# Decoder block on one core: S5's angle fractions of blocks 1 to 7 on GpSimd, another order of sums in bc's first half, and a begin with the first weight unit in halves

## The chip, the core and the metric

The kernel runs on one core of a Trainium2 chip. The metric is the device time of one execution in microseconds (us). TensorE (PE in the rows, PEld its weight loads), VectorE (DVE), ScalarE (ACT) and GpSimd (POOL) each work through a queue of their own in order and wait for one another on semaphores. SyncE (SP) issues most of the DMAs.

## The reference

A decoder block on 256 tokens of 2048 channels. The change touches the first RMSNorm with the product behind it, and the S5 mixer:

```python
hn = rmsnorm(h, norm_mix_w)
z, xbc, dt_raw, u, g_a, g_b = split(hn @ w_in)
...
def s5_mixer(u, lam_re, lam_im, log_dt, b_re, b_im, c_re, c_im, d_skip, w_glu):
    lam_bar = exp(lam * dt)                      # 64 groups x 64 states
    bu = einsum("gpc,blgc->blgp", b_bar, u)
    states = linear_scan(lam_bar, bu)            # s[t] = lam_bar * s[t-1] + bu[t]
    y = einsum("gcp,blgp->blgc", cmat, states).real + d_skip * u
    y = gelu(y)
    val, gate = split(y @ w_glu)
    return val * sigmoid(gate)
```

Then a gated merge with a Mamba-2 mixer, an output product, and a gated MLP with a short convolution.

## The kernel before, in words

**Products.** A float32 product runs as three products of parts: weights and activations are split into a high part (ScalarE's copy into the rounded type) and a low part (VectorE's subtraction). A weight unit is 512 KB, 128x1024 elements. Four of them stand in a ring: SyncE loads `raw`, ScalarE makes `whi` (`split_hi`, line 740), VectorE makes `wlo` (`split_lo`, line 1216, called `lo(j)` inside a step) and TensorE takes both, 16 matmuls for one unit in this part of the program (lines 1915 and 1917). There are 584 units, numbered from 0 here, in the phases u0 (0 to 3), u (4 to 15), zx (16 to 111), bc (112 to 143), gate and so on.

**The begin.** The four units of u0 are split in halves of 128x512 (lines 777 and 1248), and the activation is not yet normed: ScalarE and VectorE split the weighed input column by column (`weighed_hi`, line 764, and `weighed_lo`, line 1238). SyncE issues x's first quarter and then unit 0, x's second quarter and then unit 1, and so on. TensorE multiplies 17 times a tile of ones into a bank that nobody reads (line 1971) until the first halves are there. Behind u0 VectorE weighs `wdt` and adds four tiles of squares, and TensorE takes units 4 and 5.

**The S5 mixer in zx and bc.** It has 8 blocks of 4 tiles. A turn of the loop takes one block beside four groups of four units each: blocks 0 to 5 in zx, block 6 in bc's first half, block 7 in its second. Step r of a turn (`mixer_turn`) has tile r. The scan is run on inputs turned back by the angle of lam_bar, with its modulus alone (`s5_turn_back`, `s5_inputs`, `s5_scan`), and the states are turned on again (`s5_turn_on`). The tables of sines need, for each tile, the fraction of time times angle. ScalarE writes the product to `ang` and that plus a large constant to `angm` (`angles`, lines 826 and 827). Then `s5_fractions` on VectorE does `(angm - MAGIC) - ang` in one instruction (line 1359) and releases `ang_ready`. ScalarE's `sines` of the next step waits for that, behind the step's first `hi`.

The states of four tiles have to be summed with their swapped halves before TensorE takes them to y (`s5_products`, line 2010): GpSimd does tiles 0 to 2 by adding DMAs (`state_sum`, line 624), VectorE does tile 3 (`last_state_sum`, line 1398). `s5_products` of a block runs in the next turn, behind its second unit and `s5_drive` (line 1999). It waits there for the sums of the group just ended (`group_sums`, line 1221), then for `cz_ready`, `state_in` and `state_ready`.

**GpSimd's queue in a turn** is: `fill_next` (copies to `cz`, once y of the block before is there), `load_next` (a copy to `ubs` and 8 DMAs), in the turns of blocks 1 and 2 `fold`, in that of block 3 the last steps for dt, then three `state_sum`.

## Time and profile before

| | us |
|---|---|
| median of 3 runs | 1672.93 (1672.84 to 1673.79) |
| the profiled execution | 1673.03 |
| its span, first to last instruction | 1671.3 |
| TensorE busy | 1661.6 (99%) |
| VectorE busy | 1315.7 (79%) |
| ScalarE busy | 984.2 (59%) |
| GpSimd busy | 234.9 (14%) |

The time of the profiled execution is 1.7 us more than its span. TensorE is busy in every one of the page's 40 slices at 90% or more, but the last (80% to 90%), and the granted clock is 0.999 of the full one over the span. GpSimd's share leaves out its DMA issues. A view of waits tells for each engine which instruction ended its idle time; for an engine that is busy 99% of the span, those few waits are all that another order of work can take away or add.

### The profile page before, as it was taken

To read this page: it belongs to the slowest core of one execution; us is meant where nothing else is said; L and a number is where in the kernel's file an instruction comes from. 1 tells how busy PE (TensorE), PEld (TensorE's weight loads), DVE (VectorE), ACT (ScalarE), POOL (GpSimd) and SP (SyncE) were. 2 spreads that over 40 slices of the span, in tenths; PEclk is the share of its full clock that TensorE was granted. 3 is DMA by queue.
4 is the path that set the end of the run, shared out by engine and by line. 5 is a ranking of instruction groups with operands and counts; after the bars stand their busy time and mean duration, and the time that the engine had idled before them with its cause. 6 is when DMAs were issued, how large, how long until landed. Compare 5 with 4: busy or idle time off the path is not lost.

```text
span 1671.3 us, 24189 instructions
## 1 busy us (share of the span) xinstructions
PE 1661.6 (99%) x8216; PEld 1386.3 (83%) x8216; DVE 1315.7 (79%) x1723; ACT 984.2 (59%) x1365; POOL 234.9 (14%) x337
## 2 busy tenths in 40 slices
PE   9999999999999999999999999999999999999998
PEld 8888888888888888888888888888888888888886
DVE  7999999999999996545766868888878888845544
ACT  7676676666677877444547754444444454454554
POOL 7843342221111110000000200000000000000001
PEclk9999999999999999999999999999999999999999
DMA  7666766666857666666787577777777777766564
GB/s 255 214 196 197 207 202 202 191 196 180 248 201 252 218 223 205 197 192 208 243 254 223 176 233 241 237 245 243 243 244 242 243 233 243 232 190 198 191 189 127
DMA packets 182873, 361.61 MB, mean 216 GB/s; under 512 B 17520, under 2 KB 45456, under 8 KB 182672
## 3 DMA queue, kind: packets, MB, share of 16 engines
q1 hardware_dynamic: 169264, 340.23, 64.0%
q0 software_dynamic: 12336, 19.92, 5.1%
q8 instruction: 40, 0.66, 0.2%
q10 hardware_dynamic: 1200, 0.53, 0.1%
q14 instruction: 33, 0.27, 0.0%
HBM read 335.41 MB, written 18.92 MB: 212 GB/s over the span
## 4 chain that ended last, share of the span: by engine, by line
PE 74%; DVE 2%; ACT 1%; issue 0%; DVEq 0%
PE psum L1930 23%; PE psum L1931 23%; PE psum L1932 23%; PE psum L1915 2%; PE psum L1917 1%; PE psum L2051 1%; DVE wlo L1216 1%; PE psum L2052 0%; DVE dec L1566 0%; ACT whi L740 0%; PE psum L2058 0%; PE psum L1966 0%; DVE dec L1562 0%; ACT xtok L949 0%; DVE zx L1629 0%
## 5 line engine op out<-in xcount | busy, mean ns | idle before, releaser
L740 ACT ACTIVATE whi<-raw 128x1024 fp32r<-128x1024 f32 x580 | 612.6, 1058 | 583.2 <-PE psum L1932 472.0
L1216 DVE TENSOR_TENSOR wlo<-raw,whi 128x1024 fp32r<-128x1024 f32 x580 | 708.8, 1228 | 312.6 <-ACT whi L740 305.9
L1915 PE MATMUL psum<-act,whi 128*128 128x512 f32 x1088 | 342.5, 396 | 0.0
L1930 PE MATMUL psum<-whi,nw 128*128 128x512 f32 x704 | 274.1, 389 | 0.0
L1931 PE MATMUL psum<-wlo,nw 128*128 128x512 f32 x704 | 273.9, 389 | 0.0
L1932 PE MATMUL psum<-whi,nw 128*128 128x512 f32 x704 | 273.9, 389 | 0.0
L1917 PEld LDWEIGHTS psum<-act,wlo 128*128 128x128 f32 x1088 | 204.4, 188 | 48.3
L1917 PE MATMUL psum<-act,wlo 128*128 128x256 f32 x1088 | 213.7, 278 | 0.0
L1915 PEld LDWEIGHTS psum<-act,whi 128*128 128x128 f32 x1088 | 165.6, 189 | 3.3 <-issue 3.2
L1932 PEld LDWEIGHTS psum<-whi,nw 128*128 128x128 f32 x704 | 132.1, 188 | 27.6
L1930 PEld LDWEIGHTS psum<-whi,nw 128*128 128x128 f32 x704 | 132.1, 188 | 27.3
L1931 PEld LDWEIGHTS psum<-wlo,nw 128*128 128x128 f32 x704 | 132.1, 188 | 27.3
L1930 PE MATMUL psum<-whi,act 128*128 128x512 f32 x352 | 138.0, 392 | 0.0
L1930 PE MATMUL psum<-whi,ff 128*128 128x512 f32 x352 | 137.2, 390 | 0.0
L1932 PE MATMUL psum<-whi,act 128*128 128x512 f32 x352 | 137.1, 389 | 0.0
L1931 PE MATMUL psum<-wlo,act 128*128 128x512 f32 x352 | 137.1, 389 | 0.0
L1932 PE MATMUL psum<-whi,ff 128*128 128x512 f32 x352 | 137.0, 389 | 0.0
L1931 PE MATMUL psum<-wlo,ff 128*128 128x512 f32 x352 | 137.0, 389 | 0.0
L1930 PEld LDWEIGHTS psum<-whi,act 128*128 128x128 f32 x352 | 66.1, 188 | 14.1 <-issue 0.4
L1932 PEld LDWEIGHTS psum<-whi,act 128*128 128x128 f32 x352 | 66.1, 188 | 14.0
L1931 PEld LDWEIGHTS psum<-wlo,ff 128*128 128x128 f32 x352 | 66.1, 188 | 13.7
L1930 PEld LDWEIGHTS psum<-whi,ff 128*128 128x128 f32 x352 | 66.1, 188 | 13.7
(255 smaller groups left out, 2236.7 us busy)
## 6 DMA issues: line engine op xcount, KB each, us to landing
raw<-in_w_up SPq DMA_DIRECT2D x176, 512.0 KB, 4.8
raw<-in_w_zx SPq DMA_DIRECT2D x96, 512.0 KB, 3.7
raw<-in_w_down SPq DMA_DIRECT2D x88, 512.0 KB, 4.3
raw<-in_w_gate SPq DMA_DIRECT2D x64, 512.0 KB, 5.2
raw<-in_w_proj SPq DMA_DIRECT2D x48, 512.0 KB, 4.4
raw<-in_w_bc SPq DMA_DIRECT2D x32, 512.0 KB, 3.9
raw<-in_w_glu SPq DMA_DIRECT2D x32, 512.0 KB, 4.5
raw<-in_w_out SPq DMA_DIRECT2D x32, 512.0 KB, 4.7
```

Of the source, the lines that this page charges most:

```text
L740: fn(whi[:, s, :], raw[:, s, :], ACTF.Copy).then_inc(hi_ready, 1)
L1216: V.tensor_tensor(wlo[:, s, :], raw[:, s, :], whi[:, s, :], ALU.subtract).then_inc(lo_ready, 1)
L1915: mm(psum[:, b + t, :], whi[:, s, cols(t)], x, start=first, stop=False)
L1917: ins = mm(psum[:, b + t, L:2 * L], wlo[:, s, cols(t)], x[:, 0:L], start=False, stop=last)
L1930: mm(banks[:, t, :], x_hi, high[:, k], start=first and k == 0, stop=False)
L1931: mm(banks[:, t, :], x_hi, low[:, k], start=False, stop=False)
L1932: ins = mm(banks[:, t, :], x_lo, high[:, k], start=False, stop=last and k == 1)
L2051: mm(y, xtok[:, 0, x], dec[half][:, k, 0:L], start=True, stop=False)
```

## The change

Three parts.

1. **Fractions.** In blocks 1 to 7 the fraction of an angle is computed on GpSimd, in two instructions of 128x256 (`fractions`: a subtraction of the constant, a wait for it, a subtraction of two tiles), as soon as ScalarE's `angm` is there. `s5_fractions` on VectorE stays for block 0. GpSimd's queue gets four such pairs in a turn (three in the last), and `fold` and the steps for dt move behind the first `state_sum` of their turn and the pair that follows it.
2. **Sums.** At the end of bc's first half VectorE does `group_sums` ahead of `last_state_sum`, and the third low part of the step (`lo(2)`) comes behind both. In the second half the order is the old one.
3. **Begin.** SyncE issues the first half of unit 0, x's first quarter, the second half of unit 0, unit 1, x's second quarter, unit 2, and so on. ScalarE and VectorE split a half of the weights ahead of its two columns of x. TensorE's products of ones are 13 instead of 17.

```diff
+            sp.dma_start(raw[:, 0, 0:2 * L], a["w_u"][0][:, 0:2 * L]).then_inc(w_first, 16)
             for c in range(4):
                 sp.dma_start(xin[:, 4 * c:4 * c + 4, :], a["x"][:, 4 * c:4 * c + 4, :]).then_inc(x_in[c], 16)
-                sp.dma_start(raw[:, c, :], a["w_u"][c]).then_inc(w_in[c], 16)
+                if c == 0:
+                    sp.dma_start(raw[:, 0, 2 * L:], a["w_u"][0][:, 2 * L:]).then_inc(w_in[0], 16)
+                if c < 3:
+                    sp.dma_start(raw[:, c + 1, :], a["w_u"][c + 1]).then_inc(w_in[c + 1], 16)
...
+            def fractions(count):
+
+                pool.wait_ge(angm_ready, count)
+                step.done(G.tensor_scalar(angm[:, 1, :], angm[:, 0, :], MAGIC, None, ALU.subtract))
+                G.tensor_tensor(ang[:, 0, :], angm[:, 1, :], ang[:, 0, :], ALU.subtract).then_inc(ang_ready, 1)
...
+            for blk in range(1, 8):
+                fill_next(blk - 1)
+                fractions(blk * 4 + 2)
+                if blk < 7:
+                    load_next(blk)
+                state_sum(blk, 0)
+                fractions(blk * 4 + 3)
+                if blk in (1, 2):
+                    fold(2 * blk, 2 * blk)
+                if blk == 3:
+                    dt_rows()
+                state_sum(blk, 1)
+                fractions(blk * 4 + 4)
+                state_sum(blk, 2)
+                if blk < 7:
+                    fractions(blk * 4 + 5)
...
-            act.wait_ge(parm_in, 16)
             for c in range(4):
-                act.wait_ge(x_in[c], 16)
                 for half, done in ((0, half_hi), (1, hi_ready)):
+                    act.wait_ge(w_first if c == 0 and half == 0 else w_in[c], 16)
+                    w = slice(half * 2 * L, half * 2 * L + 2 * L)
+                    fn(whi[:, c, w], raw[:, c, w], ACTF.Copy).then_inc(done, 1)
+                    if c == 0 and half == 0:
+                        act.wait_ge(parm_in, 16)
+                    act.wait_ge(x_in[c], 16)
                     for k in range(4 * c + 2 * half, 4 * c + 2 * half + 2):
                         weighed_hi(k)
-                    act.wait_ge(w_in[c], 16)
-                    w = slice(half * 2 * L, half * 2 * L + 2 * L)
-                    fn(whi[:, c, w], raw[:, c, w], ACTF.Copy).then_inc(done, 1)
...
                     group_conv(*before)
+                    ends_first_half = name == "bc" and i == 0 and r == per - 1
                     s5_scan(tile, last)
-                    if not last:
+                    if not last and not ends_first_half:
                         lo(2)
                     cpad_free(*before)
                     s5_turn_on(r)
-                    if r == per - 1 and name == "bc":
+                    if last:
                         last_state_sum(blk)
                     if r == per - 1 and not last:
                         group_sums(name, i, r)
-                    if not last:
+                    if ends_first_half:
+                        last_state_sum(blk)
+                        lo(2)
+                    if start:
                         s5_fractions(blk * 4 + (r + 2))
...
-            for k in range(17):
+            for k in range(13):
                 mm(WARM, ones[:, :], ones[:, :], start=True, stop=True)
```

VectorE's loop over the four units of u0 is turned round in the same way as ScalarE's.

GpSimd in the turn of block 6 (bc's first half), before: `cz`, `ubs` and `bz` are what the next block's products need, `st` the state sums.

```order
170 L600 COPY cz<-cfold 64x8x16 x2
171 L612 COPY ubs<-ub 128x256
172 L491 DMA bz<-in_s_b 16x2x64 x8
173 L624 DMA st_75<-st_75 128x256 x2
174 L624 DMA st_76<-st_76 128x256 x2
175 L624 DMA st_77<-st_77 128x256 x2
```

And now, from the same copies to `cz` on:

```order
210 L605 COPY cz<-cfold 64x8x16 x2
211 L656 TENSOR_SCALAR angm<-angm 128x256
212 L657 TENSOR_TENSOR ang<-angm,ang 128x256
213 L617 COPY ubs<-ub 128x256
214 L496 DMA bz<-in_s_b 16x2x64 x8
215 L629 DMA st_75<-st_75 128x256 x2
216 L656 TENSOR_SCALAR angm<-angm 128x256
217 L657 TENSOR_TENSOR ang<-angm,ang 128x256
218 L629 DMA st_76<-st_76 128x256 x2
219 L656 TENSOR_SCALAR angm<-angm 128x256
220 L657 TENSOR_TENSOR ang<-angm,ang 128x256
221 L629 DMA st_77<-st_77 128x256 x2
```

Four pairs are new; the fourth stands behind these rows.

VectorE at the end of bc's first half, before, from the scan of the last step to the next step's first instruction:

```order
256 L1387 SCALAR_TENSOR_TENSOR sx<-s5k,sx 128x256 x2
257 L1216 TENSOR_TENSOR wlo<-raw,whi 128x1024
258 L1392 TENSOR_TENSOR st_78<-sx,tab_71 128x1024
259 L1398 TENSOR_TENSOR st_78<-st_78 128x512
260 L1221 TENSOR_TENSOR cpad<-psum,hsum 128x2x256
261 L1359 SCALAR_TENSOR_TENSOR ang<-angm,ang 128x256
262 L1216 TENSOR_TENSOR wlo<-raw,whi 128x1024 x2
263 L1368 TENSOR_TENSOR rot<-psum,tab_70 128x1024
```

And now:

```order
249 L1403 SCALAR_TENSOR_TENSOR sx<-s5k,sx 128x256 x2
250 L1408 TENSOR_TENSOR st_78<-sx,tab_71 128x1024
251 L1236 TENSOR_TENSOR cpad<-psum,hsum 128x2x256
252 L1414 TENSOR_TENSOR st_78<-st_78 128x512
253 L1231 TENSOR_TENSOR wlo<-raw,whi 128x1024 x3
254 L1384 TENSOR_TENSOR rot<-psum,tab_70 128x1024
```

One low part went behind the two sums, the sums changed places, and the fraction is gone.

## Rows read from the trace of the kernel before

**Rows 1.** Waits of TensorE, 340 to 500 us: line, releaser, total us, times, longest.

```profile
PE psum L2010 <- DVE cpad L1221: 0.4, 1, 0.4
```

**Rows 2.** Stretch: length, busy us of PE, PEld, DVE, ACT, POOL; clock; DMA.

```profile
297.00:344.00 47.00, 47.00 (x296) 40.11 (x288) 44.42 (x58) 32.15 (x53) 11.63 (x17) 1.00 0.68 199
344.00:391.00 47.00, 47.00 (x292) 40.11 (x288) 46.52 (x68) 31.61 (x52) 11.68 (x17) 1.00 0.65 190
```

**Rows 3.** Timeline, first 8 us: start, duration, engine, line, operation, tiles, [idle before].

```profile
1.07 5.47 PE L1971 MATMUL psum<-ones 128*128 128x128 f32 x34 [1.07 <-POOL dtp L483]
...
5.04 0.91 ACT L764 ACTIVATE nw<-xin,parm 128x256 fp32r<-128x256 f32 x2 [2.26 <-DMA parm<-in_parm]
...
5.67 0.88 DVE L1238 SCALAR_TENSOR_TENSOR nw<-xin,parm,nw 128x256 fp32r<-128x256 f32 x2 [5.67 <-ACT nw L764]
...
6.92 0.69 DVE L1248 TENSOR_TENSOR wlo<-raw,whi 128x512 fp32r<-128x512 f32 x1 [0.37 <-ACT whi L777]
...
7.76 0.70 PE L1915 MATMUL psum<-nw,whi 128*128 128x512 f32 x2 [1.21 <-DVE wlo L1248]
```

**Rows 4.** The DMA issues of x (first) and of units 0 to 3.

```profile
L382 SPq DMA_DIRECT2D xin<-in_x x4: 400/480/627, 0.8 to 4.5; - x4
...
DMA to landing us min/median/max: 4.0/6.3/8.2
...
L383 SPq DMA_DIRECT2D raw<-in_w_u x4: 415/442/468, 1.3 to 5.2; - x4
...
DMA to landing us min/median/max: 5.0/7.0/8.9
```

**Rows 5.** Timeline, the end of u0 up to TensorE's first matmul of unit 5.

```profile
16.04 3.88 ACT L761 ACTIVATE xsq<-xin 128x1024 f32<-128x1024 f32 x4
...
17.61 1.23 DVE L1250 TENSOR_TENSOR wdt<-wdt,parm 128x1024 f32<-128x1024 f32 x1
...
26.14 0.81 PE L1915 MATMUL psum<-nw,whi 128*128 128x512 f32 x2
```

**Rows 6.** Timeline, where bc's first half ends; 392.41 is unit 130.

```profile
389.75 0.69 DVE L1398 TENSOR_TENSOR st<-st 128x512 f32<-128x512 f32 x1
...
390.36 0.68 DVE L1221 TENSOR_TENSOR cpad<-psum,hsum 128x512 f32<-128x512 f32 x1
...
391.41 1.07 PE L2010 MATMUL psum<-st,cz 128*32 128x256 f32 x16 [0.41 <-DVE cpad L1221]
...
392.41 0.74 PE L1915 MATMUL psum<-act,whi 128*128 128x512 f32 x2
```

**Rows 7.** Timeline, unit 142 in bc's second half: its low part, its first matmul.

```profile
424.53 1.20 DVE L1216 TENSOR_TENSOR wlo<-raw,whi 128x1024 fp32r<-128x1024 f32 x1
...
425.98 0.40 PE L1915 MATMUL psum<-act,whi 128*128 128x512 f32 x1
```

**Rows 8.** Timeline of VectorE in block 2's turn, while GpSimd folds.

```profile
166.89 0.84 DVE L1359 SCALAR_TENSOR_TENSOR ang<-angm,ang 128x256 f32<-128x256 f32 x1
...
171.50 1.21 DVE L1368 TENSOR_TENSOR rot<-psum,tab 128x1024 f32<-128x1024 f32 x1
```

**Rows 9.** Timeline of VectorE in block 5's turn, with no fold.

```profile
299.22 1.31 DVE L1216 TENSOR_TENSOR wlo<-raw,whi 128x1024 fp32r<-128x1024 f32 x1
...
306.65 0.41 DVE L1359 SCALAR_TENSOR_TENSOR ang<-angm,ang 128x256 f32<-128x256 f32 x1
306.99 2.35 DVE L1216 TENSOR_TENSOR wlo<-raw,whi 128x1024 fp32r<-128x1024 f32 x2
```

**Rows 10.** Timeline of GpSimd in the stretch of rows 8: two of the fold's seven instructions.

```profile
167.53 0.80 POOL L526 TENSOR_TENSOR cfold<-ctmp 128x256 f32<-128x256 f32 x1
...
171.55 0.86 POOL L592 TENSOR_SCALAR ctmp<-ctmp 128x256 f32<-128x256 f32 x1
```

**Rows 11.** Timeline of ScalarE in block 5's turn: `angm` written, `ang` taken.

```profile
311.15 0.42 ACT L827 ACTIVATE angm<-ang 128x256 f32<-128x256 f32 x1
...
318.99 0.40 ACT L831 ACTIVATE ang<-ang 128x256 f32<-128x256 f32 x1
```

More of the change, by code:

```diff
@@ L237, in sem @@
             return ctx.enter_context(nc.semaphore(name))
+        w_first = sem("w_first")
         x_in, w_in = [[sem(f"{n}{k}") for k in range(4)] for n in ("x_in", "w_in")]
@@ L646, in _ @@
             state_sums(0)
-            fill_next(0)
-            load_next(1)
-            fold(2, 2)
-            state_sums(1)
-            fill_next(1)
-            load_next(2)
-            fold(4, 4)
-            state_sums(2)
-            fill_next(2)
-            load_next(3)
-            horner_steps((7, 5, 3))
-            step.done(G.tensor_scalar(series, series, 1.0, 2.0, ALU.add, ALU.mult))
-            mul(series, series, ratio)
-            step.done(G.tensor_scalar(square, dtx[0:DT, :], 0.0, None, ALU.max))
@@ L661, in _ @@
-            mul(dt, series, square, ALU.add)
-            G.tensor_scalar(ratio, dt, dtp[0:DT, 2:3], -1.0, ALU.mult, ALU.mult).then_inc(dt_row, 1)
-            pool.wait_ge(dt_row, 1)
-            for k, at_k in ((0, 0), (1, P)):
-                pool.dma_start(scr[:, at_k:at_k + P], dtw[64 * k:64 * k + HEADS, 0, :]).then_inc(scr_w, 16)
-            state_sums(3)
-            fill_next(3)
-            for blk in range(4, 7):
-                load_next(blk)
-                state_sums(blk)
-                fill_next(blk)
@@ L672, in _, with dt_rows @@
-            state_sums(7)
+            def fractions(count):
+                pool.wait_ge(angm_ready, count)
+                step.done(G.tensor_scalar(angm[:, 1, :], angm[:, 0, :], MAGIC, None, ALU.subtract))
+                G.tensor_tensor(ang[:, 0, :], angm[:, 1, :], ang[:, 0, :], ALU.subtract).then_inc(ang_ready, 1)
+            def dt_rows():
+                horner_steps((7, 5, 3))
+                step.done(G.tensor_scalar(series, series, 1.0, 2.0, ALU.add, ALU.mult))
+                mul(series, series, ratio)
+                step.done(G.tensor_scalar(square, dtx[0:DT, :], 0.0, None, ALU.max))
+                mul(dt, series, square, ALU.add)
+                G.tensor_scalar(ratio, dt, dtp[0:DT, 2:3], -1.0, ALU.mult, ALU.mult).then_inc(dt_row, 1)
+                pool.wait_ge(dt_row, 1)
+                for k, at_k in ((0, 0), (1, P)):
+                    pool.dma_start(scr[:, at_k:at_k + P], dtw[64 * k:64 * k + HEADS, 0, :]).then_inc(scr_w, 16)
@@ L1239, in weighed_lo @@
                                        ALU.mult, ALU.subtract).then_inc(xwlo_ready, 1)
-            dve.wait_ge(parm_in, 16)
             for c in range(4):
                 for half, ready, done in ((0, half_hi, half_lo), (1, hi_ready, lo_ready)):
-                    for k in range(4 * c + 2 * half, 4 * c + 2 * half + 2):
-                        weighed_lo(k)
                     dve.wait_ge(ready, c + 1)
@@ L1248, in _ @@
                     V.tensor_tensor(wlo[:, c, w], raw[:, c, w], whi[:, c, w], ALU.subtract).then_inc(done, 1)
+                    if c == 0 and half == 0:
+                        dve.wait_ge(parm_in, 16)
+                    for k in range(4 * c + 2 * half, 4 * c + 2 * half + 2):
+                        weighed_lo(k)
             dve.wait_ge(wdt_in, 64)
```

## Prediction

> **What bounds the kernel now.** I read the waits of TensorE first. The engine is busy 99% of the span, so only its waits can be won or lost. In the part that the change touches there are two: 1.21 us ahead of its first product [rows 3], and 0.4 us where bc's first half ends [rows 1]. A third, of 0.2 us at 497 us, lies behind the change and moves with it. Then the busy times by stretch [rows 2]: in a zx turn VectorE is busy 44.4 of 47 us, in bc's first half 46.5 of 47. So zx hides some 2.5 us of added VectorE time in a turn, and bc hides almost none. Last the timeline, for how long before TensorE's first matmul of a unit its low part was ready. Two units have almost no margin: unit 142, whose low part ends at 424.53 + 1.20 = 425.73 and whose first matmul starts at 425.98, a margin of 0.25 us [rows 7], and unit 5, which starts as VectorE finishes it (below). Behind 500 us TensorE waits for nothing until the end, so what the start and bc give is the result.
>
> **The begin, the first product.** 512 KB take about 1.4 us: x's first quarter is issued at 0.8 and lands 4.0 later, at 4.8, unit 0 is issued at 1.3 and lands 5.0 later, at 6.3 [rows 4]. With half a unit ahead of it (0.7 us) x's quarter lands at 5.5. The first half of the weights is then there and split, as it lands more than 1 us earlier and its two instructions take some 1.3 us. From x: ScalarE's weighed part to VectorE's is 5.67 - 5.04 = 0.63, VectorE's own takes about half of 0.88, and VectorE to TensorE was 7.76 - (6.92 + 0.69) = 0.15 [rows 3]. That gives 5.5 + 0.63 + 0.45 + 0.15 = 6.8 instead of 7.76: about 0.9 us earlier. The 4 products of ones that go are at most 4/17 of 5.47, 1.3 us [rows 3]. They lie ahead of that wait, so they cost and give nothing, and the pause ahead of the first product stays 1.2 to 1.5 us.
>
> **The begin, what is late next.** The gain has to get past unit 5. VectorE splits eight halves with their columns, then weighs `wdt` from 17.61 on, sums squares and makes the low parts of units 4 and 5. That is a row of work with hardly a gap, and TensorE starts unit 5 at 26.14, 8.53 us behind 17.61 [rows 5]. Does 17.61 move? The new order begins VectorE's first column at about 5.5 + 0.65 = 6.15, and the second half of unit 0 (lands at 6.3, ScalarE needs 0.6) at 7.1. From there eight halves go at VectorE's pace: `wdt` started 17.61 - 6.92 = 10.7 after the first low half, and eight pairs of columns had to be done then. Now seven low halves and seven pairs are left at 7.1, with a wait of about 0.4 for x's second quarter, which now lands behind two units of weights. Seven times 1.4 and 0.4 is 10.2, so `wdt` starts at about 17.3 to 17.4. But ScalarE is later: its squares began at 16.04 [rows 5], and now stand behind x's last quarter, which lands where unit 3 did, at 5.2 + 8.9 = 14.1 [rows 4]; with its last half and four columns behind that (2.2 us) they begin at 16.3. The high part of unit 4 comes behind them, 0.25 later than before, and takes back half of VectorE's gain. I take **0.1 us gained** (0.4 lost to 0.4 gained). S5's parameters on GpSimd begin 1.3 us later, as `s5in` lands behind one more unit; their first user had more room than that.
>
> **The fraction on VectorE.** It costs the next instruction's start less its own: 306.99 - 306.65 = 0.34 us [rows 9]. GpSimd's pair comes early enough: `angm` is there at 311.15 + 0.42, `ang` is taken at 318.99 [rows 11]. Even behind two DMA issues of 0.9 us each the pair of some 1.7 us has 3 us left, and with `fold` ahead of the next one over 3. GpSimd then has nothing that TensorE waits for: `state_sum` and `load_next` move by 2 to 8 us and are needed a turn later.
>
> **The price of the pair.** The trace shows that GpSimd's work lengthens VectorE's. Beside the fold's subtraction of two tiles, 128x256 [rows 10], `ang` took 0.84 us [rows 8], and without one 0.41 [rows 9]: 0.43 more. Five of the fold's seven instructions of that width do so, each to the VectorE instruction behind it, by 0.37 to 0.53. The other two ran beside instructions that read PSUM, such as `rot` with 1.21 us [rows 8], and cost nothing. A copy of the same width, one input, made a low part 1.31 [rows 9] instead of 1.20 [rows 7]: 0.1. A pair is one instruction of each kind: 0.43 + 0.1 = 0.53. Some subtractions of the constant will fall beside PSUM readers, so I take **c = 0.5 us** for a pair. Bounds: 0.1 (only the copy's price) and 0.86 (twice the price of two inputs). So each step of VectorE becomes 0.16 longer, not 0.34 shorter. zx hides that (0.6 us in a turn).
>
> **The Trainium skill speaks harder against it.** "SBUF — State Buffer", section "Who interferes with whom", says that a VectorE instruction with two SBUF inputs and a GpSimd one that reads SBUF exclude each other for a whole instruction. By that a pair would cost VectorE 0.80 + 0.86 = 1.66 us, the durations in [rows 10]. The trace agrees on which instructions are hit (rot, with one input in PSUM, is not), but 0.43 for an instruction of 0.80 is only half of it.
>
> **Where bc's first half ends.** Before, VectorE's two sums end at 390.36 + 0.68 = 391.04 and TensorE goes on at 391.41 [rows 6]. The low part moved behind takes 1.12 (one start to the next) with it, less 0.08 as the scan's result is now waited for: 390.0. The turn has 4 pairs and, ahead of this point, 3 fractions less: 4c - 3 x 0.34 = +0.98, so 391.0. TensorE waits last for `state_ready` now and starts 0.1 later, at 391.1, 0.3 earlier than before; the low part of unit 130 ends at 391.0 + 1.1 = 392.1, and TensorE takes it at 392.2 instead of 392.41. **0.25 us gained**, and TensorE arrives that much earlier at what follows.
>
> **Bc's second half.** VectorE isn't waited for by its own inputs there, so it keeps its delay. Until unit 142's low part (third step) there are 7 pairs and 6 fractions less: 7c - 2.04 + 0.08 = 1.54. The low part ends at 425.73 + 1.54 = 427.27, and TensorE, there since 425.7, starts at 427.32 instead of 425.98: **1.34 us lost**, in place of everything gained just before. What comes behind (units 143 and 145) has more room, since the third fraction is gone then too. The gate's chain starts from TensorE and moves with it. The third wait stays.
>
> **Sum.** 1.34 less 0.12 of the begin is 1.2 us. The profiled execution took 1673.03; the runs' median is 0.1 lower. Forecast **1674.1 us**. Generally the shift is 7c - 2.28, or, where that is below -0.6, -0.6.
>
> **Rivals.**
> - *The pair costs VectorE less than it saves* (c under 0.33). For it: the copy's 0.1, and short VectorE instructions in a row may absorb more than long ones. Against: `ang` itself is a short one. At c = 0.25 unit 142 has no wait, both waits shrink, and the shift is -0.1 of the begin and -0.5 of the wait at 391: -0.6. 1672.3 to 1672.9 us.
> - *The begin keeps its 0.7 to 0.9 us*, because unit 5 comes early too. Then 0.6 less, 1673.5 us with c = 0.5. Against: the squares, which are later.
> - *Slower by over 0.2%: GpSimd takes VectorE's time in bc at the full price.* From c = 0.8 on the shift is 3.3 us; with both instructions at 0.43, c = 0.86, it is 3.7 and 1676.7 us, at unit 142. By whole durations, c = 1.66, bc gives 9.3, and a zx turn's 44.4 [rows 2] would grow by 4 x 1.32 to 49.7 of 46.9: five turns of 2.8 less the room of some 3, in all about 20 us, 1693 us. That is what the page's rule would give. Against: the 0.43.
> - *The clock falls in the pause of the begin.* The granted clock of the span is 0.999 with a pause as long. u0 at the lower level would cost 2 to 4 us: 1677 us.
> - *The change does not do what it says*: the wait at 391 stays since `state_ready` is as late as the sum was. Within the forecast's range.
>
> **Chances.** Forecast (c of 0.35 to 0.75, shift 0.2 to 3): 52%. Cheap pair: 27%. Begin kept: 8%. Full price, over 3.35 us: 8%, of which the page's rule 2%. Clock: 3%. Others: 2%. Two runs of this kernel can be told apart from about 0.2%, 3.3 us. No case wins that much, as all waits of TensorE in reach are 1.2 + 0.5 us: faster 1%, same 90%, slower 9%. The range leaves out half of the best of the cheap cases and the slow ones: 1672.3 to 1675.8.
>
> **What would show it.** In the new profile: TensorE's first product at 6.8, unit 5 at about 26.0; `ang` on GpSimd at 0.8 us or less with the VectorE instruction behind it longer by 0.4; VectorE busier in bc by 0.16 a step; no wait at 391, and a new one of 1 to 2 us in front of a low part (line 1231 there) between 410 and 430. Wrong would be: no such wait, or waits of ScalarE on `ang` from GpSimd.

## The result and the profile after

The changed kernel takes **1676.69 us** (median of 19 runs, 1676.05 to 1677.57), the kernel before 1673.10 us beside it (19 runs, 1672.63 to 1674.09): a ratio of 1.0020, 95% interval 1.0014 to 1.0026. That is slower by 3.6 us, just past the 0.2% (3.3 us) that I had set as the edge of "no change". The forecast was 1674.1 with a range up to 1675.8, so the time lies outside it. The profiled execution's span is 1674.5 us, that of before 1671.3: 3.2 us more. I use these 3.2 us for the accounting. One of the eleven executions of an experiment below, the begin alone, took 3390.96 us, twice the usual time, and is left out of the ratio there as a slow run.

The waits of TensorE over the whole span (line, releaser, total us, times, longest):

```profile
PE psum L1935 <- DVE nw L1253: 1.2, 2, 0.7
...
PE psum L1935 <- DVE wlo L1231: 0.9, 1, 0.9
PE psum L2030 <- DVE st L1414: 0.6, 1, 0.6
PE psum L1935 <- DVE ub L1438: 0.6, 1, 0.6
...
PE psum L2071 <- DVE dec L1594: 0.3, 1, 0.3
```

The wait of 1.21 ahead of the first product [rows 3] is now 0.71, but a second one of 0.51 follows. The 0.41 at 391 [rows 6] has not gone: it is 0.65. Two new waits stand in bc's second half, on `ub` and on the low part of unit 142. The last one is the forecast's "new wait of 1 to 2 us in front of a low part", with 0.89 us a little under it. Here are TensorE's rows in order of time:

```profile
7.04 0.73 PE L1935 MATMUL psum<-nw,whi 128*128 128x512 f32 x2 [0.71 <-DVE nw L1253]
10.64 0.74 PE L1935 MATMUL psum<-nw,whi 128*128 128x512 f32 x2 [0.51 <-DVE nw L1253]
...
392.31 1.07 PE L2030 MATMUL psum<-st,cz 128*32 128x256 f32 x16 [0.65 <-DVE st L1414]
399.82 0.49 PE L1935 MATMUL psum<-act,whi 128*128 128x512 f32 x1 [0.63 <-DVE ub L1438]
428.93 0.72 PE L1935 MATMUL psum<-act,whi 128*128 128x512 f32 x2 [0.89 <-DVE wlo L1231]
```

The stretches of [rows 2], with the same columns:

```profile
297.00:344.00 47.00, 47.00 (x296) 40.26 (x296) 45.78 (x55) 31.97 (x53) 19.25 (x25) 1.00 0.68 197
344.00:391.00 47.00, 47.00 (x296) 40.27 (x292) 46.15 (x63) 31.30 (x52) 20.49 (x25) 1.00 0.66 187
```

In zx VectorE is busy 1.4 us more in a turn (45.78 for 44.42), although its four fractions are gone. In bc it was full already, and fullness says nothing there; what counts is how far it falls behind. For that I follow the start of TensorE's work on each weight unit, after less before:

| unit | where | TensorE later by, us |
|---|---|---|
| 0 | first product | -0.72 |
| 5 | second unit behind u0 | +0.68 |
| 129 | end of bc's first half | +0.66 |
| 130 | behind the sums | +0.94 |
| 132 | behind `ub` | +1.70 |
| 142 | third step of bc's second half | +2.95 |
| 165 | gate | +3.41 |
| 200 to the end | | +3.21 |

So three places make the loss: the begin 0.66, bc 2.29 up to unit 142, and 0.46 behind it (0.10 at unit 143, the rest in the gate's first units), of which 0.2 comes back later. All these are differences of two single executions. How far two of them differ by themselves shows where nine kernels of the experiments below keep the old begin: their unit 5 stands -0.10 to +0.29 from the kernel before. A shift of 0.3 us at one place is therefore no finding by itself.

VectorE's convolution in a step of bc, GpSimd's pair beside it, and the low part of unit 142 behind it:

```profile
423.48 3.09 DVE L1428 SCALAR_TENSOR_TENSOR bc<-cpad,parm,bc 128x256 f32<-128x256 f32 x6
...
422.71 1.57 POOL L656 TENSOR_SCALAR angm<-angm 128x256 f32<-128x256 f32 x1 [2.91 <-ACT angm L842]
424.37 0.73 POOL L657 TENSOR_TENSOR ang<-angm,ang 128x256 f32<-128x256 f32 x1
...
427.67 1.20 DVE L1231 TENSOR_TENSOR wlo<-raw,whi 128x1024 fp32r<-128x1024 f32 x1
```

In the kernel before the same six instructions of the convolution took

```profile
359.80 2.46 DVE L1412 SCALAR_TENSOR_TENSOR bc<-cpad,parm,bc 128x256 f32<-128x256 f32 x6
```

That is **0.63 us for a pair**, where I had taken 0.5. The one-input instruction takes 1.57 us here, not the 0.86 of [rows 10]: GpSimd is held up as well. A view of the line alone (shortest/median/longest instruction in ns), before and after, shows that the loss is no general slowing:

```profile
L1412 DVE SCALAR_TENSOR_TENSOR bc<-cpad,parm,bc x6: 476/476/478, 421.0 to 423.0; 128x256 f32<-128x256 f32 x6
...
L1428 DVE SCALAR_TENSOR_TENSOR bc<-cpad,parm,bc x6: 472/474/960, 423.5 to 426.1; 128x256 f32<-128x256 f32 x6
```

Four of the six take what they took before. One takes 0.96 us, 0.48 more; it starts 0.05 behind GpSimd's instruction of two inputs (424.42 and 424.37). The first of the six takes 0.62, 0.14 more; it runs while GpSimd's instruction of one input does (422.71 to 424.28).

The pair ahead of the first step of bc's second half runs earlier in the step, at 395.90 and 396.84. The convolution takes 2.45 there, and the low part ahead of it takes 1.76 us, 0.54 more than the 1.22 of the same one before:

```profile
397.44 1.76 DVE L1231 TENSOR_TENSOR wlo<-raw,whi 128x1024 fp32r<-128x1024 f32 x1
```

### The profile page after: what moved, and what is told of

It reads as the page before. It is cut to its first block, busy times and chain, and to the rows that moved or that the text cites. A ratio compares the mean times of both kernels' runs of the same rounds, so it can differ in the third digit from the quotient of the medians.

```text
span 1674.5 us, 24201 instructions
## 1 busy us (share of the span) xinstructions
PE 1662.9 (99%) x8208; PEld 1386.7 (83%) x8208; DVE 1323.0 (79%) x1696; ACT 983.2 (59%) x1365; POOL 293.1 (18%) x391
## 4 chain that ended last, share of the span: by engine, by line
PE 93%; DVE 4%; ACT 2%; issue 1%; DMA 0%; SPq 0%; DVEq 0%; ACTq 0%
PE psum L1950 23%; PE psum L1951 23%; PE psum L1952 23%; PE psum L1935 15%; PE psum L1937 7%; DVE wlo L1231 1%; DVE bc L1428 1%; PE psum L2071 1%; ACT whi L754 1%; PE psum L2019 0%; PE psum L2030 0%; DMA xin<-in_x 0%; DVE dec L1586 0%; PE psum L2072 0%; DVE rot L1384 0%
```

## The parts by themselves

Four kernels took the change apart. The theory behind them: begin and fractions each cost time, the sums win something that unit 142 takes back.

**The begin alone.** The kernel before, with the begin's edits (the half unit first, 13 products of ones, weights ahead of columns on ScalarE and VectorE):

```diff
+            sp.dma_start(raw[:, 0, 0:2 * L], a["w_u"][0][:, 0:2 * L]).then_inc(w_first, 16)
             for c in range(4):
                 sp.dma_start(xin[:, 4 * c:4 * c + 4, :], a["x"][:, 4 * c:4 * c + 4, :]).then_inc(x_in[c], 16)
-                sp.dma_start(raw[:, c, :], a["w_u"][c]).then_inc(w_in[c], 16)
+                if c == 0:
+                    sp.dma_start(raw[:, 0, 2 * L:], a["w_u"][0][:, 2 * L:]).then_inc(w_in[0], 16)
+                if c < 3:
+                    sp.dma_start(raw[:, c + 1, :], a["w_u"][c + 1]).then_inc(w_in[c + 1], 16)
...
-            for k in range(17):
+            for k in range(13):
```

> The kernel before with the new begin alone. Theory 1 (the losses add up along TensorE's queue): unit 5 starts 0.68 us later than in the kernel before, as in the changed kernel, every later unit keeps that, since VectorE is led by TensorE in zx, and the span is 1671.95 us (+0.65). Theory 2 (the begin's loss is made good later, as zx and bc have their own waits): unit 16 on is where it was, 1671.3 us, and all of the 3.2 us come from bc.

Measured: 1674.05 us beside 1673.15 for before, ratio 1.0005 (0.9996 to 1.0014). Unit 0 starts 0.69 earlier, unit 4 0.15 later, unit 5 0.53 later, and the end is 0.29 later. Neither theory has it whole: TensorE keeps about 0.5 up to unit 180, as Theory 1 says, and gets 0.2 back behind it. The changed kernel gets as much back in the same place. The time alone can't be told from no change, but the trace can: the 0.7 us won at unit 0 have become a loss of half a microsecond at unit 5.

**Everything but the begin** (the old begin with the fractions and the sums):

```diff
-            for k in range(13):
+            for k in range(17):
```

and the begin's other lines likewise as they were.

> The changed kernel with the old begin: fractions on GpSimd and the new order at the end of bc's first half. Theory 1: with 0.63 us for a pair (six convolution instructions of VectorE took 3.08 us beside a pair, 2.45 before) unit 142's low part is 7 x 0.63 - 6 x 0.34 + 0.08 = 2.45 us late, TensorE 2.2 to 2.3 there, and with some 0.35 in the gate the span is 1673.9 us (+2.6). Theory 2: all of it, 1674.5 us.

Measured: 1675.84, ratio 1.0017 (1.0008 to 1.0026). TensorE is level at unit 129 (+0.08), then +0.36 at 130, +1.13 at 132, +2.37 at 142, +2.84 at 165 and +2.62 at the end. This is Theory 1, with the span of 1673.9 us that it gave. So 2.6 of the 3.2 us come from fractions and sums together. By the medians begin and rest add up (0.9 and 2.7 are the measured 3.6), by the spans of the profiled executions 0.3 and 2.6 make 2.9 of 3.2; the begin's own interval, -0.7 to +2.3 us, is too wide to choose.

**The fractions alone** (old begin, old order of the sums):

```diff
-                    if not last:
+                    if start:
                         s5_fractions(blk * 4 + (r + 2))
```

with GpSimd's new loop over blocks 1 to 7.

> The kernel before with the fractions of blocks 1 to 7 on GpSimd, nothing else. Theory 1: at the end of bc's first half the sums end 4 x 0.63 - 3 x 0.34 = 1.5 us later and TensorE waits about 2 us there instead of 0.5; at unit 142 VectorE is 2.4 late, so the order of the sums decides only where the time is lost: 1673.8 us (+2.5). Theory 3 (the low part behind the sums is what costs, by the waits at units 130 and 132): under 1673.0 us.

Measured: 1676.31, ratio 1.0017 (1.0008 to 1.0026); the end is 3.33 later, more than the 2.5 of Theory 1; Theory 3 is out. Nearly all of it comes at one place: -0.11 at unit 129, +1.82 at unit 130 and +2.92 from unit 131 on. The first number is the wait on the sums:

```profile
PE psum L2019 <- DVE cpad L1230: 1.9, 1, 1.9
```

The second I had not expected. TensorE works there and is still late. The stretches around it (length, busy us of PE, PEld, DVE, ACT, POOL, granted clock, DMA):

```profile
391.00:393.00 2.00, 0.23 (x5) 0.20 (x9) 1.97 (x4) 2.00 (x5) 0.00 (x0) 1.00 0.75 250
393.00:396.50 3.50, 3.50 (x22) 2.30 (x15) 3.46 (x5) 1.90 (x5) 1.88 (x4) 0.53 0.45 157
396.50:400.00 3.50, 3.50 (x21) 3.05 (x20) 3.50 (x7) 1.06 (x1) 0.66 (x1) 0.98 0.63 193
```

Behind a wait of 1.9 us the granted clock is 0.53 for 3.5 us, about the lower of its two levels (1.2 GHz for 2.4), and that costs 1.1 us (unit 130 at +1.82, unit 131 at +2.92). At unit 142 there is no wait here, since TensorE itself comes later than that low part.

**The sums alone** (old begin, VectorE's fractions):

```diff
+                    ends_first_half = name == "bc" and i == 0 and r == per - 1
                     s5_scan(tile, last)
-                    if not last:
+                    if not last and not ends_first_half:
                         lo(2)
...
-                    if r == per - 1 and name == "bc":
+                    if last:
                         last_state_sum(blk)
                     if r == per - 1 and not last:
                         group_sums(name, i, r)
+                    if ends_first_half:
+                        last_state_sum(blk)
+                        lo(2)
```

> The kernel before with the new order of sums alone. Theory 1: the wait of 0.5 us at 391 goes, but unit 142 has a margin of 0.25, so 0.1 to 0.2 us is left at the end: 1671.1 to 1671.2 us. Rival: the wait's 0.5 us is won, 1670.8 us. Other rival: units 130 or 132 wait for the low part or for the output behind it, 1671.5 us or more.

Measured: 1673.39, ratio 1.0002 (0.9993 to 1.0011). The wait at 391 is gone: unit 129 is at +0.15, unit 130 at -0.33, so 0.48 is won. Unit 142 is at +0.14, and the end at +0.36. The sums do what the change says, and it is all given back. The span is 1671.7 us, above the 1671.1 to 1671.2 of Theory 1; the second rival named such a time, but not for this reason, as TensorE waits at neither unit 130 nor unit 132.

## What a pair on GpSimd costs VectorE

In these kernels VectorE keeps its fraction. GpSimd works in the changed kernel's order, and in place of each fraction it makes instructions of the same width whose result nobody reads. They cost what they cost VectorE, and save nothing.

**The pair, unused:**

```diff
                 pool.wait_ge(angm_ready, count)
-                step.done(G.tensor_scalar(angm[:, 1, :], angm[:, 0, :], MAGIC, None, ALU.subtract))
-                G.tensor_tensor(ang[:, 0, :], angm[:, 1, :], ang[:, 0, :], ALU.subtract).then_inc(ang_ready, 1)
+                step.done(G.tensor_scalar(angm[:, 1, :], iota[:, :], MAGIC, None, ALU.subtract))
+                step.done(G.tensor_tensor(angm[:, 1, :], iota[:, :], iota[:, :], ALU.subtract))
```

> The kernel before, where VectorE keeps its fraction, with GpSimd's work in the changed kernel's order and, in place of each fraction there, a pair of the same kinds and width (128x256, one of one input and one of two) on operands of no use, one written to a buffer that nobody reads. It measures what the pair costs VectorE without what the fraction saves. Theory 1 (c = 0.63 us for a pair): VectorE's steps in bc 12.5 to 12.7 us instead of 12.01 where TensorE doesn't hold it, the six instructions of the convolution 3.0 to 3.1 instead of 2.46, and 7 pairs less the 0.25 of room at unit 142: 4.2 us in all, to which zx may add some, since 4 pairs are 2.5 us and its turn has about 2.5 of room: 1677.0 to 1678.5. Theory 2 (the pair is cheap, and the changed kernel's loss is that its wait for GpSimd's sums or order moved): steps within 0.2, 1673.0 to 1675.0. Theory 3 (a pair excludes VectorE for its whole 1.66 us): over 1690.

Measured: 1677.53, ratio 1.0027 (1.0017 to 1.0037). VectorE's convolution and GpSimd's second instruction:

```profile
373.35 2.96 DVE L1421 SCALAR_TENSOR_TENSOR bc<-cpad,parm,bc 128x256 f32<-128x256 f32 x6
...
374.23 0.61 POOL L652 TENSOR_TENSOR angm<-iota 128x256 f32<-128x256 f32 x1
```

The convolution takes 0.50 more than the 2.46 of before, and the step is 12.51 instead of 12.01 (360.84 to 373.35). A pair that excluded VectorE for its whole length would have given over 1690 us (Theory 3). But 0.50 is not the 0.63 of the changed kernel. GpSimd's instruction is shorter too, 0.61 for 0.74. Hence the next three.

**One kind at a time, and two tiles.** The first leaves out the instruction of two inputs, the second that of one, the third lets the one of two inputs read two different tiles:

```diff
-                step.done(G.tensor_tensor(angm[:, 1, :], iota[:, :], iota[:, :], ALU.subtract))
+                step.done(G.tensor_tensor(angm[:, 1, :], angm[:, 1, :], iota[:, :], ALU.subtract))
```

> As the run with the unused pair, but only the instruction of one input (subtract a constant, 128x256) per step on GpSimd; VectorE keeps its fraction. With the unused pair the six instructions of the convolution took 2.96 us instead of 2.46, and VectorE's step 12.51 instead of 12.01. Theory 1 (both kinds cost, the one of two inputs most, as the prediction's 0.1 and 0.43): convolution 2.5 to 2.6, step 12.05 to 12.15. Theory 2 (an instruction of one input costs as much as one of two): 2.70 and 12.25. Theory 3 (only that of two inputs costs): 2.46 and 12.01.

> The same with only the instruction of two inputs (128x256, both inputs the same tile). Theory 1: convolution 2.80 to 2.90, step 12.35 to 12.45. Theory 2: 2.70 and 12.25. Theory 3: 2.96 and 12.5. Here it begins earlier than behind the other one, so a part of it may fall beside VectorE's instructions that read PSUM and cost nothing: then below 2.7.

> The unused pair again, but the instruction of two inputs reads two different tiles, as the changed kernel's does, where the first unused pair read one tile twice. There GpSimd's instruction took 0.61 us and cost VectorE, with the other one, 0.50; in the changed kernel it took 0.72 to 0.74 and the pair cost 0.63. Theory 1 (it is the second tile: what GpSimd's instruction takes longer, VectorE loses too): GpSimd 0.72 to 0.74, convolution 3.09, step 12.64, and the total 0.9 us (7 x 0.13) above the first unused pair's 1677.5. Theory 2 (it is that the changed kernel's VectorE has no fraction, or the place in the step): 0.61, 2.96, 12.51, and 1677.5 again.

The convolution in the three, one input alone, two inputs alone, and the pair with two tiles:

```profile
371.98 2.60 DVE L1420 SCALAR_TENSOR_TENSOR bc<-cpad,parm,bc 128x256 f32<-128x256 f32 x6
```

```profile
372.31 2.81 DVE L1420 SCALAR_TENSOR_TENSOR bc<-cpad,parm,bc 128x256 f32<-128x256 f32 x6
```

```profile
363.58 3.08 DVE L1421 SCALAR_TENSOR_TENSOR bc<-cpad,parm,bc 128x256 f32<-128x256 f32 x6
...
364.46 0.73 POOL L652 TENSOR_TENSOR angm<-angm,iota 128x256 f32<-128x256 f32 x1
```

One input costs 0.14 (2.60 - 2.46), two inputs from the same tile 0.35 (2.81 - 2.46), together 0.49: the 0.50 of the unused pair. With two tiles GpSimd's instruction takes 0.73 and the pair costs 0.62, the price in the changed kernel. So the second tile is the missing 0.13. By difference an instruction of two inputs from two tiles costs 0.48, and that is what the one long instruction of the convolution had lost in the changed kernel's own trace. This is Theory 1 of each (the first at the edge of its 2.5 to 2.6), but for the third one's total time.

The Trainium skill ("SBUF — State Buffer", section "Who interferes with whom") says that a VectorE instruction with two SBUF inputs contends with a GpSimd one that reads SBUF, and that the ports they share are an exclusive lock. The traces agree on the partners and that both engines are held up. They do not show VectorE shut out for the length of a GpSimd instruction: one of 0.73 us cost 0.48, and one of 1.57 us with one input cost 0.14.

One run each gave 1673.61 and 1674.64 us for the first two, and for the third 1680.86, where I had expected 1678.4. It loses more than seven pairs in bc, since four pairs are 2.5 us in a turn of zx and use up its room (TensorE is 3.16 late at unit 129 already), and since the clock falls behind the wait at 394:

```profile
394.00:396.00 2.00, 0.15 (x4) 0.00 (x0) 1.97 (x3) 0.97 (x2) 0.00 (x0) 1.00 0.37 90
396.00:398.00 2.00, 0.97 (x13) 0.61 (x16) 2.00 (x4) 0.88 (x3) 0.00 (x0) 0.85 0.43 172
398.00:400.00 2.00, 2.00 (x12) 1.20 (x5) 2.00 (x3) 2.00 (x4) 0.91 (x2) 0.50 0.41 94
```

**Fractions on GpSimd in zx alone.** VectorE makes those of blocks 6 and 7; new sums, old begin:

```diff
-                    if start:
+                    if not last and (start or name == "bc"):
                         s5_fractions(blk * 4 + (r + 2))
...
-                fractions(blk * 4 + 2)
+                if blk < 6:
+                    fractions(blk * 4 + 2)
```

> The changed kernel's fractions on GpSimd in zx alone (blocks 1 to 5), VectorE makes them in bc (blocks 6 and 7), with the new order of sums and the old begin. Theory 1 (the pair costs VectorE more than the fraction in both phases, zx hides it, bc does not): as the run with the sums alone, unit 129 within 0.1 us of before, 0.2 to 0.4 earlier at unit 130 and back to +0.1 to +0.4 at unit 143: 1672.7 to 1673.7. Theory 2 (the loss comes from the GpSimd order, its sums and loads moved by up to 8 us, or from clock or memory traffic over the whole of the phase): 1 us or more remains, over 1674.2.

Measured: 1673.23, ratio 1.0000 (0.9991 to 1.0010). Unit 129 at +0.20, unit 130 at -0.29, unit 142 at +0.18, the end at +0.16: the sums alone over again. Twenty pairs in zx cost nothing, while fractions and sums together, with seven pairs in bc more, cost 2.3 us up to unit 142. GpSimd's moved sums, loads and `fold` in zx are innocent, as they are moved in this kernel too. Those of bc are not tested by themselves; among the waits of TensorE in the changed kernel none is on one of GpSimd's sums.

## Why the begin loses

**The halves alone.** Unit 0 comes in two transfers of 2 KB a row at its old place:

```diff
-                sp.dma_start(raw[:, c, :], a["w_u"][c]).then_inc(w_in[c], 16)
+                if c == 0:
+                    sp.dma_start(raw[:, 0, 0:2 * L], a["w_u"][0][:, 0:2 * L]).then_inc(w_first, 16)
+                    sp.dma_start(raw[:, 0, 2 * L:], a["w_u"][0][:, 2 * L:]).then_inc(w_in[0], 16)
+                else:
+                    sp.dma_start(raw[:, c, :], a["w_u"][c]).then_inc(w_in[c], 16)
```

> The kernel before, with the first weight unit's transfer in two halves of 2 KB a row at its old place, behind x's first quarter; ScalarE's first half waits for the first of them. Everything else as before. Theory A (rows of half the length cost transfer time): what lies behind the halves lands later than in the kernel before, x's second quarter at 7.9 to 8.3 us instead of 7.51 and x's last at 13.2 to 13.5 instead of 12.76, and unit 5 starts 0.3 to 0.6 us later. Theory B (the order of the transfers costs it: a whole unit now stands ahead of x's second quarter): landings within 0.15 us of before, unit 5 within 0.1 us of 26.14 or up to 0.3 earlier, as the first half is split 0.3 us sooner.

**The order alone.** The new begin, with unit 0 whole and first:

```diff
-            sp.dma_start(raw[:, 0, 0:2 * L], a["w_u"][0][:, 0:2 * L]).then_inc(w_first, 16)
+            sp.dma_start(raw[:, 0, :], a["w_u"][0]).then_inc(w_in[0], 16)
...
-                if c == 0:
-                    sp.dma_start(raw[:, 0, 2 * L:], a["w_u"][0][:, 2 * L:]).then_inc(w_in[0], 16)
```

> The new begin's order of transfers and of work on ScalarE and VectorE, but with the first weight unit whole and first, in one transfer. Theory A (short rows): x's second quarter lands at 8.8 to 9.0 us, 0.6 earlier than the 9.5 of the changed kernel, so unit 5 is at 26.1 to 26.4. Theory B (order): it lands at 9.0 to 9.5, the columns of x's second quarter wait for it as in the changed kernel, and unit 5 is at 26.6 to 27.0. Both expect TensorE's first product at 7.3 to 7.7, as x's first quarter now lands behind a whole unit.

**x's quarters ahead of their units again**, with the halves:

```diff
-                if c < 3:
-                    sp.dma_start(raw[:, c + 1, :], a["w_u"][c + 1]).then_inc(w_in[c + 1], 16)
+                else:
+                    sp.dma_start(raw[:, c, :], a["w_u"][c]).then_inc(w_in[c], 16)
```

and on ScalarE and VectorE the columns ahead of the weights from the second half of unit 0 on.

> The new begin with the halves, but x's second, third and fourth quarters each ahead of the weight unit that they go with, as in the kernel before, and the columns ahead of the weights from the second half of unit 0 on. If the late landing of x's second quarter behind a whole unit is what costs the begin its gain, it lands at 7.8 to 8.1 us instead of 9.5, VectorE has no idle time from 6.5 us on, wdt starts at 17.0 to 17.4 (18.27 in the changed kernel, 17.61 before), and unit 5 at 25.7 to 26.2. If it is the halving, or ScalarE's squares behind the last quarter, unit 5 stays at 26.5 or later.

What came out, from one profiled execution each (a transfer has landed when the last of its 16 parts has):

| kernel | x's 2nd quarter lands | x's last | `wdt` starts | unit 0 | unit 5 |
|---|---|---|---|---|---|
| before | 7.51 | 12.76 | 17.61 | 7.76 | 26.14 |
| halves alone | 7.80 | 13.40 | 17.54 | -0.29 | +0.30 |
| order alone | 8.82 | 14.18 | 17.84 | -0.26 | +0.22 |
| x ahead, halves | 8.48 | 13.76 | 18.21 | -0.37 | +0.65 |
| after | 9.53 | 14.91 | 18.27 | -0.72 | +0.68 |

The nine other kernels with the old begin have x's second quarter at 7.37 to 7.82, x's last at 12.65 to 13.05, the squares at 15.97 to 16.32, `wdt` at 17.49 to 17.89 and unit 5 at -0.10 to +0.29. So the loss of the begin at unit 5 is clear of what executions differ by: +0.53, +0.65 and +0.68 in the three kernels that have the halves first. The +0.30 of the halves and the +0.22 of the order are not, one execution each; that they add up to 0.52 may be chance, and how the loss divides between the two is not shown.

What the halves do to the transfers is clearer. x's last quarter lands at 13.40, as Theory A said (13.2 to 13.5), and the squares begin at 16.70, both outside of what the others show. x's second quarter, at 7.80, is under Theory A's 7.9 and among the others. With the unit whole and first it lands at 8.82 (Theory A: 8.8 to 9.0). The delay is in the last parts: in the kernel before the 16 parts of x's last quarter land from 12.32 to 12.76, with the halves alone from 12.27 to 13.40. They are 0.44 apart before, 0.42 to 0.74 in the nine others, 0.72 with the order alone, and 1.13, 1.36 and 0.98 in the other three rows of the table. Theory B's mechanism does not show: with a whole unit ahead of it x's second quarter lands at 8.82, and VectorE has no idle time behind it. What the order does move is ScalarE's squares: they begin at 16.39 instead of 16.04, as they now stand behind x's last columns. In the third kernel x's second quarter landed at 8.48, not at 7.8 to 8.1, VectorE waits for the weights behind it instead, and unit 5 is at 26.79: the second outcome of its text (26.5 or later). That row, and three of the changed kernel:

```profile
10.46 0.69 DVE L1263 TENSOR_TENSOR wlo<-raw,whi 128x512 fp32r<-128x512 f32 x1 [0.50 <-ACT whi L787]
```

```profile
8.99 0.69 DVE L1260 TENSOR_TENSOR wlo<-raw,whi 128x512 fp32r<-128x512 f32 x1 [0.17 <-ACT whi L787]
10.10 0.88 DVE L1253 SCALAR_TENSOR_TENSOR nw<-xin,parm,nw 128x256 fp32r<-128x256 f32 x2 [0.42 <-ACT nw L778]
...
18.27 1.27 DVE L1266 TENSOR_TENSOR wdt<-wdt,parm 128x1024 f32<-128x1024 f32 x1
```

In the halves alone `wdt` is even 0.07 earlier and unit 5 still 0.30 later, and ScalarE is late: its squares begin at 16.70 instead of 16.04 [rows 5] and VectorE waits 0.41 for the high part of unit 4 behind them. In the changed kernel they begin at 17.07. So both engines' rows count, and each new order moved one of them. "The order alone" ends within 0.06 of before, so it loses nothing that one execution can show, and it wins nothing. The halves alone lose 0.5 more in one wait at 46.7 us, on a later `ub`; I did not find its cause. By time the three can't be told from the kernel before: one run each gave 1673.80, 1673.09 and 1673.82 us, and the kernel before beside them 1672.81 to 1673.43.

## Is it one low part, or VectorE's whole row

The sums win 0.48 and lose it at unit 142. In the next kernel, the sums alone with one more edit, that low part goes ahead of the scans, in each step of bc's second half but the last:

```diff
+                    ahead = name == "bc" and i == 1 and not last
+                    if ahead:
+                        lo(2)
                     s5_scan(tile, last)
-                    if not last and not ends_first_half:
+                    if not last and not ends_first_half and not ahead:
                         lo(2)
```

> The new order of sums alone, and in bc's second half the third low part of a step goes ahead of the scans. With the sums alone TensorE won 0.48 us at unit 130 and gave all of it back at unit 142, whose low part ended 0.06 before its first matmul. Theory A (that one low part's place is the limit): unit 142 keeps the gain, and the end is 0.3 to 0.5 us earlier than before. Theory B (VectorE's whole row in bc is the limit, and stands 0.35 us later than before for all low parts from unit 131 on): unit 142 keeps it, but units 143 and 145, whose low parts stand behind the scans and have 0.3 to 0.4 of room, give it back; the end is within 0.15 us of before.

Measured in one run each: 1675.19 beside 1673.64, span 1673.4. Unit 142 keeps the gain (-0.24). Unit 143 is at +0.72, unit 147 at +1.01, unit 158 at +2.33, the end at +2.13. Theory A is out, and the loss is far over the 0.15 us that Theory B allowed. VectorE's rows show why:

```profile
421.86 2.46 DVE L1412 SCALAR_TENSOR_TENSOR bc<-cpad,parm,bc 128x256 f32<-128x256 f32 x6
424.23 1.22 DVE L1216 TENSOR_TENSOR wlo<-raw,whi 128x1024 fp32r<-128x1024 f32 x1
425.37 1.27 DVE L1387 TENSOR_TENSOR_SCAN sx<-s5k,sx 128x256 f32<-128x256 f32 x2
426.74 1.23 DVE L1392 TENSOR_TENSOR st<-sx,tab 128x1024 f32<-128x1024 f32 x1
```

From the scans' start to the next instruction's it is 1.37 us here (425.37 to 426.74). With the sums alone it is 1.18 (423.69 to 424.87), because there the low part comes next, which doesn't need the scan's result. The step is 12.22 (409.63 to 421.86) instead of 12.01, and there is no spare time in it. Beyond unit 147 a late `xtok` adds a wait of 0.7. So the edit did not only move the low part, it also made VectorE's row longer: three such steps are some 0.6 us (an estimate, 3 x 0.21) of the 0.96 that TensorE loses between units 142 and 143. The remaining third is about what Theory B gives back. That VectorE's row as a whole is the limit, and not one place in it, fits these numbers, but this kernel alone does not prove it. None of these kernels beats the one before, so I ran no combination.

## Where the prediction was right and where wrong

That a loss shows as a wait on the low part of unit 142 was forecast rightly, the time was not. Two steps failed: the price of a pair, put at 0.5 us and measured at 0.63 (0.95 us of the miss of 2.0), and the start of unit 5 behind the new begin, put at a gain of 0.1 and measured as a loss of 0.66 to 0.68 (0.78 us of it).

**The begin, the first product: right in kind.** 6.8 forecast, 7.04 measured. x's first quarter landed at 5.78 instead of 5.5.

**The begin, unit 5: wrong, by 0.8 us.** The step that failed is "`wdt` starts at about 17.3 to 17.4" and the "0.1 us gained" behind it. It started at 18.27, and unit 5 at 26.82 instead of 26.0. I had sized the wait for x's second quarter at 0.4; with what the halves add to it, it and the one ahead of it were 0.59, the row began 0.2 later (7.33 for 7.1), and seven pairs and halves took 10.35 us, 0.55 more than seven times 1.4. Together that is the 0.97 from 17.3 to 18.27. I had also put the squares at 16.3; they began at 17.07, because x's last quarter landed at 14.91 and not at 14.1. Behind the late landings is the step "512 KB take about 1.4 us", which I used for halves too. With the order alone x's last quarter lands at 14.18, about where that step puts it (14.1); the halves add 0.73 to it there, and 0.64 to the old order. Why the row itself took 0.55 longer isn't shown.

**The fraction on VectorE and GpSimd's room: right but for one step.** Of its 27 takings of an `ang` from GpSimd, ScalarE waits at one, for 0.15 us at 237 us. The forecast had named such waits as a sign of being wrong; this one costs TensorE nothing (+0.65 at unit 16, +0.66 at unit 129).

**The pair's price: the term was mis-sized.** c is 0.63 (0.14 for one input, 0.48 for two from two tiles), not 0.5. The row of the fold's subtraction had given 0.43 and that of the copy 0.1. I had worked out 0.43 + 0.1 = 0.53 and rounded it down, for pairs beside instructions that read PSUM. No pair in bc was so lucky: six of the seven stand beside the convolution, and the one at 396 us hits a low part for 0.54.

**bc's first half: right in mechanism, wrong in sign by the same term.** With c = 0.63 four pairs cost 0.52 more than with 0.5; -0.25 becomes +0.27, and 0.28 was measured (unit 129 to 130). The rival that "the wait at 391 stays" came true. TensorE waits for `state_ready` there, as that rival says, but only because the pairs ahead make VectorE's sums late: without the fractions on GpSimd the wait does go.

**The wait on `ub` at unit 132, 0.6 to 0.8 us, I had not seen.** It costs nothing in the end, as unit 142 lies behind it.

**Unit 142: the formula holds.** The low part ends at 428.87, 3.14 later than before, 0.66 of it from the begin, so 2.48; 7 x 0.63 - 2.04 + 0.08 is 2.45. That it comes so close is in part luck: one of the seven pairs cost 0.54, and the new order of sums costs VectorE's row some 0.18 and not 0.08 (13.31 for 13.13 us from one convolution to the next with the sums alone). With c = 0.5 it was 1.54. That is 0.9 us of the error.

**"What comes behind moves with it": not quite.** From 142 to 165 TensorE loses 0.46 more and later gets 0.2 back. With the fractions alone, where TensorE itself was late, it lost 0.37 in the same units; with the unused pair, none. From 461 us on VectorE's work in the gate stands 3.41 behind, 0.36 more than TensorE. Which input sets that, I can't say from the traces.

**The sum.** Forecast +1.2, measured +3.2 on the span. The miss of 2.0 is 0.78 from the begin, 0.95 in bc (7 x 0.13 = 0.91 of it from c) and 0.26 from what lies behind unit 142. **The rivals:** the "full price" rival, with its result of 1676.7, came closest in time. It is not what happened: its condition was c over 0.8, and c is 0.63, with the begin on top. "The clock falls" was put at the begin, where it did not; in a part of the change run alone it fell at 391.

## What to carry over

Take work off a full engine onto GpSimd only when the price beside it is smaller than the saving: here 0.63 us paid for 0.34 saved. In the trace of before, two of the fold's instructions beside VectorE's PSUM readers had cost nothing; whether the pair can be placed there was not tried. Price each instruction by the number of different tiles that it reads, and don't round a per-step price that the sum multiplies by seven. Where a transfer is split to start something earlier, follow everything that lands behind it, on each engine that it feeds, up to the first place where TensorE has no room.

## What the runs showed of the hardware

- The price on VectorE of a GpSimd instruction of 128x256 beside its two-input instructions: 0.14 us with one input, 0.35 with both inputs from one tile, 0.48 from two tiles. The first two add up (0.50 for the pair). In the changed kernel each of the two prices falls on one instruction of VectorE, which takes 0.62 or 0.96 us instead of 0.48.
- TensorE's clock fell behind one wait inside a busy stretch (one profiled execution of each kernel). Behind idle times of 1.9 us (fractions alone), 2.4 (unused pair) and 2.9 (two tiles) the granted clock was 0.50 to 0.53 of full for some 3 us, with 0.7 to 1.1 us lost; behind 1.6 us (two inputs alone) it stayed at 1.00. The rows of that last kernel:

```profile
391.00:392.00 1.00, 0.00 (x0) 0.00 (x0) 1.00 (x2) 0.00 (x0) 0.00 (x0) 1.00 0.87 250
392.00:393.00 1.00, 0.41 (x8) 0.34 (x12) 1.00 (x3) 0.32 (x1) 0.00 (x0) 1.00 0.54 217
393.00:394.00 1.00, 1.00 (x17) 0.52 (x7) 1.00 (x2) 1.00 (x4) 0.17 (x1) 1.00 0.00 0
```

 and those of the unused pair:

```profile
393.00:394.00 1.00, 0.08 (x4) 0.11 (x8) 1.00 (x3) 0.00 (x0) 0.00 (x0) 1.00 0.77 311
394.00:395.00 1.00, 1.00 (x12) 0.64 (x15) 1.00 (x2) 0.99 (x4) 0.00 (x0) 0.50 0.02 8
```

 In the execution with 1.9 a wait longer by 0.3 us than the 1.6 cost a microsecond more; two executions set no bound between them. Here the new order of the sums may pay: with it the wait is 0.65 and the clock stays, and fractions with sums end 0.7 us earlier than fractions alone in the profiled executions (+2.62 and +3.33). By the medians it is 0.5 (1675.84 and 1676.31), and the two ranges overlap.
- A unit sent as two transfers with rows of 2 KB moved x's last quarter, six transfers behind it, by 0.64 us (13.40 for 12.76; 12.65 to 13.05 in nine other executions), and its 16 parts landed 1.13 us apart instead of 0.44 (0.42 to 0.74 in the nine).
